# Rotary halves swapped by a TensorE permutation matmul instead of by DMA

## The reference, cut to what matters

```python
def rotary(x):                       # x: (batch, token, head, 64)
    ...
    x1, x2 = xf[..., : d // 2], xf[..., d // 2 :]
    return jnp.concatenate([x1 * cos - x2 * sin, x1 * sin + x2 * cos], axis=-1)

rq = rotary(r_q.reshape(B, S, RET_HEADS, RET_QK_DIM))
rk = rotary(r_k.reshape(B, S, RET_HEADS, RET_QK_DIM))
y_ret = head_groupnorm(retention(rq, rk, ...))
```

## Time and profile before

| | |
|---|---|
| median of three runs | 1784.98 us (1782.87 to 1786.29) |
| the profiled execution's own time | 1786.29 us |
| its span | 1784.6 us |
| PE busy | 1704.8 us, 96% of the span |
| DVE, ACT, POOL busy | 463.6, 387.2, 105.0 us |
| DMA, whole span | 502.70 MB, 282 GB/s |

### The profile page before, as it was taken

One profiled execution on the slowest core, in us unless ns is written; L12 is line 12 of the kernel. 1 busy time (PEld: TensorE's weight loads), 2 busy tenths in 40 slices (PEclk: granted clock), 3 DMA queues, 4 the chain that ended last, 5 costly groups with the idle time before them and its releaser, 6 DMA issues.

```text
span 1784.6 us, 36430 instructions
## 1 busy us (share of the span) xinstructions
PE 1704.8 (96%) x15726; PEld 954.2 (53%) x15726; DVE 463.6 (26%) x868; ACT 387.2 (22%) x604; POOL 105.0 (6%) x191
## 2 busy tenths in 40 slices
PE   7989999999999997999999999999999999999986
PEld 5767887888788766434434343434333343343333
DVE  4354527325544344561000000000000000010015
ACT  5464323333334325001001010100000000000011
POOL 0011000000000011000000000000000000000012
PEclk9999999999999999899999999999999999999998
DMA  7202421233225332999999999999999999999995
GB/s 240 71 24 76 155 98 39 87 102 142 95 94 190 118 95 102 407 396 399 390 410 397 411 398 411 399 409 399 411 410 400 411 409 403 410 408 404 411 417 218
DMA packets 105105, 502.70 MB, mean 282 GB/s; under 512 B 11191, under 2 KB 21575, under 8 KB 55457
## 3 DMA queue, kind: packets, MB, share of 16 engines
q1 hardware_dynamic: 83904, 461.40, 65.5%
q0 software_dynamic: 8192, 26.37, 4.8%
q10 hardware_dynamic: 12864, 12.72, 2.0%
HBM read 486.25 MB, written 14.81 MB: 281 GB/s over the span
## 4 chain that ended last, share of the span: by engine, by line
PE 66%; SPq 18%; DMA 8%; DVE 3%; ACT 2%; issue 2%; POOL 1%; another core or an unknown queue 0%; ACTq 0%; DVEq 0%
PE ps L1982 18%; SPq L504 18%; PE ps L2006 9%; PE ps L1669 9%; PE ps L1671 9%; PE ps L1670 9%; DMA work<-in_w_exp_in 7%; PE ps L1766 1%; PE ps L1813 1%; PE ps L1833 1%; PE ps L486 1%; PE ps L1940 1%; PE ps L1973 1%; PE ps L1950 1%; DMA raw<-in_w_in 1%
## 5 line engine op out<-in xcount | busy, mean ns | idle before, releaser
L1982 PE MATMUL ps<-ring,moe 128*32 128x512 f32 x3808 | 416.2, 594 | 3.2 <-DMA ring<-in_w_exp_in 3.2
L1982 PEld LDWEIGHTS ps<-ring,moe 128*32 128x32 f32 x3808 | 115.6, 110 | 289.7 <-issue 257.2
L1564 DVE TENSOR_SCALAR moe<-ps 128x768 f32<-128x768 f32 (+1 forms) x32 | 28.0, 874 | 847.4 <-PE ps L1982 847.4
L2006 PE MATMUL ps<-ring,moe 128*32 128x256 f32 x3648 | 202.6, 379 | 0.2 <-DMA ring<-in_w_exp_out 0.2
L1095 DVE TENSOR_TENSOR wl<-raw,wh 128x1024 fp32r<-128x1024 f32 x104 | 126.0, 1224 | 250.5 <-ACT wh L746 250.5
L746 ACT ACTIVATE wh<-raw 128x1024 fp32r<-128x1024 f32 x104 | 109.0, 1057 | 244.1 <-PE ps L1671 243.5
L2006 PEld LDWEIGHTS ps<-ring,moe 128*32 128x32 f32 x3648 | 110.8, 110 | 82.5 <-DMA ring<-in_w_exp_out 1.0
L1669 PE MATMUL ps<-oph,wh 128*128 128x512 f32 x384 | 150.9, 393 | 2.4 <-DVE work L1227 1.6
L1670 PE MATMUL ps<-opl,wh 128*128 128x512 f32 x384 | 149.7, 390 | 0.0
L1671 PE MATMUL ps<-oph,wl 128*128 128x512 f32 x384 | 149.6, 390 | 0.0
L988 ACT ACTIVATE moe<-ps 128x768 f32<-128x768 f32 (+1 forms) x32 | 23.8, 744 | 579.2 <-DVE moe L1564 579.2
(11 more groups left out here) (327 smaller groups left out, 1686.2 us busy)
## 6 DMA issues: line engine op xcount, KB each, us to landing
ring<-in_w_exp_in SPq DMA_DIRECT2D x172, 1024.0 KB, 28.0
ring<-in_w_exp_out SPq DMA_DIRECT2D x86, 1024.0 KB, 28.9
moe<-in_w_exp_in SPq DMA_DIRECT2D x43, 1024.0 KB, 28.1
work<-in_w_exp_in SPq DMA_DIRECT2D x41, 1024.0 KB, 28.0
raw<-in_w_in SPq DMA_DIRECT2D x26, 1024.0 KB, 5.4
work<-in_w_exp_out SPq DMA_DIRECT2D x22, 1024.0 KB, 29.8
moe<-in_w_exp_out SPq DMA_DIRECT2D x20, 1024.0 KB, 27.9
raw<-in_w_ckv SPq DMA_DIRECT2D x8, 1024.0 KB, 5.0
```

Source lines behind the costliest of these rows:

```text
L1564: nc.vector.tensor_scalar(act_n[:, 0:g], ps[:, 0:g, 256:512].rearrange("p j (n a) -> p j a n", a=2), 1.0 - LIMIT, 1.0 + LIMIT, ALU.max, AL ...
L1982: ins = nc.tensor.matmul(ps[32 * s:32 * s + 32, j, :], xt[:, k, 32 * j:32 * j + 32], w[:, s, :, :], start=False, stop=(k == KT - 1), tile_ ...
L2006: ins = nc.tensor.matmul(y_bank(s, j), at[:, a, j, q, :], w[:, a, s, :], start=False, stop=(q == W2 - 1 and a == 1), tile_position=(0, 32 ...
```

## The change

POOL's eight swap DMAs, their semaphores and the buffers `q_swap` and `k_swap` are gone. A tenth constant matrix, `rot_swap` (128 x 128, loaded with the two matrices of stick-breaking attention, so that this load is 192 KB and no longer 128 KB), has one entry of 1 or -1 in each column; multiplied with a tile of q or k it gives the swapped halves with their signs, and the sine table loses its signs. PE does this product for the eight tiles, in plain float32, right behind `rk` and ahead of `rv0`, into banks 4 to 7: tiles 0 to 3 are q, tiles 4 to 7 are k, and tile `u` of k waits until DVE has finished the sum of tile `u - 4` in the same bank. All eight stand behind a wait for ACT's last eviction of `rk` and one for the last low part of the stick-breaking output (`o_lo`). DVE takes one tile at a time: the product of the swapped tile, read from PSUM, with the sine into a scratch tile of two (`rot_tmp`), the product with the cosine, a wait for both, and the sum. ACT's wait at the first gate tile is gone. The constants behind the new matrix move up by one place.

```diff
-    sine = np.concatenate([-np.sin(ang), np.sin(ang)])
-    rot = np.stack([np.tile(np.cos(ang), (4, 1)), np.tile(sine, (2, 1))]).astype(np.float32)
+    rot = np.stack([np.tile(np.cos(ang), (4, 1)), np.tile(np.sin(ang), (4, 1))]).astype(np.float32)
...
+    for m in range(P):
+        d = m % 64
+        mats[3, m + 32 if d < 32 else m - 32, m] = -1.0 if d < 32 else 1.0
...
-        q_swap, k_swap = view(8704, 4, T), view(10752, 4, T)
+        rot_tmp = view(1024, 2, T)
...
-            pool.dma_start(w_(14976, 2 * P).rearrange("p (c n) -> p c n", c=2),
-                           c_mats[1:3].rearrange("c p n -> p c n")).then_inc(in_neg, 16)
+            pool.dma_start(w_(14976, 3 * P).rearrange("p (c n) -> p c n", c=3),
+                           c_mats[1:4].rearrange("c p n -> p c n")).then_inc(in_neg, 16)
...
-            for n, (dst, src) in enumerate(((q_swap, q_r), (k_swap, k_r))):
-                pool.wait_ge(tile_out["act"], 16 + 4 * n)
-                for b in range(4):
-                    a = 32 * (b ^ 1)
-                    pool.dma_start(dst[32 * b:32 * b + 32], src[a:a + 32]).then_inc(swapped[n], 16)
...
-                    if n == 0 and t == 0:
-                        act.wait_ge(rot_out, 8)
...
-            for n, (part, other) in enumerate(((q_r, q_swap), (k_r, k_swap))):
-                dve.wait_ge(swapped[n], 64)
-                for u in range(4):
-                    nc.vector.tensor_tensor(other[:, u, :], other[:, u, :], sine, ALU.mult).then_inc(rot_part, 1)
-                    nc.vector.tensor_tensor(part[:, u, :], part[:, u, :], cosine, ALU.mult).then_inc(rot_part, 1)
-                for u in range(4):
-                    dve.wait_ge(rot_part, 8 * n + 2 * u + 2)
-                    nc.vector.tensor_tensor(part[:, u, :], part[:, u, :], other[:, u, :], ALU.add).then_inc(rot_out, 1)
+            for u in range(8):
+                v = (q_r, k_r)[u // 4][:, u % 4, :]
+                dve.wait_ge(rot_done, u + 1)
+                if u >= 2:
+                    dve.wait_ge(rot_out, u - 1)
+                chain(nc.vector.tensor_tensor(rot_tmp[:, u % 2, :], ps[:, 4 + u % 4, :], sine, ALU.mult))
+                chain(nc.vector.tensor_tensor(v, v, cosine, ALU.mult))
+                chain.wait()
+                nc.vector.tensor_tensor(v, v, rot_tmp[:, u % 2, :], ALU.add).then_inc(rot_out, 1)
...
             project("rk", op_h, op_l)
+            pe.wait_ge(tile_out["act"], 20)
+            for u in range(8):
+                if u >= 4:
+                    pe.wait_ge(rot_out, u - 3)
+                elif u == 0:
+                    pe.wait_ge(o_lo, PAIRS)
+                nc.tensor.matmul(ps[:, 4 + u % 4, :], rot_swap, (q_r, k_r)[u // 4][:, u % 4, :], start=True,
+                                 stop=True).then_inc(rot_done, 1)
             for name in ("rv0", "rv1", "rg0"):
                 project(name, op_h, op_l)
...
             pe.wait_ge(rot_out, 8)
-            pe.wait_ge(o_lo, PAIRS)
             retention_scores(0)
```

More of the change, by code:

```diff
@@ L147, in constant_tables @@
     i = np.arange(P)
-    mats = np.zeros((9, P, P), np.float32)
+    mats = np.zeros((10, P, P), np.float32)
     mats[0] = np.eye(P)
@@ L151, in constant_tables @@
     mats[2] = -1.0
[L152 to L155, removed]
+    for m in range(P):
+        d = m % 64
+        mats[3, m + 32 if d < 32 else m - 32, m] = -1.0 if d < 32 else 1.0
+    mats[4] = i[:, None] < i[None, :]
+    mats[5] = 1.0
+    mats[6] = i[None, :]
+    mats[7] = (i[:, None] % NE) == (i[None, :] % NE)
     for g in (2, 3):
@@ L164, in constant_tables @@
                 break
-        mats[10 - g, :, order] = np.arange(32 * g)[:, None]
+        mats[11 - g, :, order] = np.arange(32 * g)[:, None]
     inv = np.float32(10000.0) ** (-np.arange(0, 64, 2, dtype=np.float32) / np.float32(64))
     ang = (np.arange(T, dtype=np.float32)[None, :] * inv[:, None]).astype(np.float32)
-    sine = np.concatenate([-np.sin(ang), np.sin(ang)])
-    rot = np.stack([np.tile(np.cos(ang), (4, 1)), np.tile(sine, (2, 1))]).astype(np.float32)
+    rot = np.stack([np.tile(np.cos(ang), (4, 1)), np.tile(np.sin(ang), (4, 1))]).astype(np.float32)
     u = np.arange(2 * P)[None, :] - i[:, None]
@@ L242, in view @@
             return w_(a, tiles * n).rearrange("p (t n) -> p t n", t=tiles)
-        neg_from, neg_ones = (w_(14976 + P * n, P) for n in range(2))
+        neg_from, neg_ones, rot_swap = (w_(14976 + P * n, P) for n in range(3))
         x_nat = view(0, TT, D)
@@ L390, in layer_kernel @@
         ln_done, neg_ready, soft_hi, soft_lo = (sem(n) for n in ("ln_done", "neg_ready", "soft_hi", "soft_lo"))
-        swapped, rot_part, rot_out = [sem("q_swapped"), sem("k_swapped")], sem("rot_part"), sem("rot_out")
+        rot_done, rot_out = sem("rot_done"), sem("rot_out")
         sc_done, sc_out, ro_done, ro_out = (sem(n) for n in ("sc_done", "sc_out", "ro_done", "ro_out"))
@@ L616, in _ @@
             pool.wait_ge(xo_done, 2 * XH)
-            pool.dma_start(mats2, c_mats[3:7].rearrange("c p n -> p c n")).then_inc(in_moe, 16)
+            pool.dma_start(mats2, c_mats[4:8].rearrange("c p n -> p c n")).then_inc(in_moe, 16)
             pool.dma_start(names["brt"], b_router[0].partition_broadcast(P)).then_inc(in_moe, 16)
@@ L638, in _ @@
             pool.wait_ge(rt_ready, 3)
-            pool.dma_start(mats2[:, 0:2, :], c_mats[7:9].rearrange("c p n -> p c n")).then_inc(in_fill, 16)
+            pool.dma_start(mats2[:, 0:2, :], c_mats[8:10].rearrange("c p n -> p c n")).then_inc(in_fill, 16)
             def gather_rows(g):
```

## The result

The changed kernel takes 1797.47 us (median of 8 runs, 1791.52 to 1800.96) against 1786.12 us for the kernel before (8 runs): a ratio of 1.0054, 95% interval 1.0041 to 1.0067. In two later sets of runs it was 1.0062 (1.0045 to 1.0078) and 1.0058 (1.0039 to 1.0077). The change costs 10 to 12 us. One more execution of the changed kernel, taken with the first measurement, ran for 2953.05 us at a mean granted clock of 0.557; it belongs to a slow state of the chip, and no number here uses it. The profiled execution has a span of 1794.9 us, 10.3 more than before.

A forecast was written before the change was run, and what follows sets the result against it. PE was taken to bound the rotary stretch, with no idle time. Swaps of 6.9 us and waits of 3.9 us made 10.8 us, added to the 1784.98 us median for 1795.8 us; range 1792.5 to 1799.5 us.

The forecast's parts named there:

- The sum: PE from rk to rv0: 6.9 us of swaps plus 3.9 us of waiting, 10.8 us slower.
- Rival B: Swap stretch on PE: the clock falls as well, 1.5 us more, 12.3 us slower; chance 0.42 together with D.
- D: PE's queue at the swaps: each hand-over costs 0.3 us more, 12.3 us slower; chance 0.42 together with Rival B.
- A: The sum as it stands: 10.8 us slower, TensorE's clock unchanged; chance 0.52.
- What bounds: Rotary stretch, 166.8 to 254 us: PE never idle, so its time is paid at once; removing the swap DMAs gives 0.
- Step 1: PE behind rk: waits for ACT's last copy, first swap at 189.62 us; 0.8 us of waiting.
- Step 2: Each swap on PE, a float32 product of 128 x 128 with 512 columns: 0.86 us.
- Steps 3 and 4: DVE's rotation: starts about 1.2 us after the first swap, then takes 1.93 us for each tile.
- Steps 5 and 6: Last swap on PE waits for DVE's fourth sum; rv0 starts at 199.6 us, a loss of 10.8 us.
- What is queued behind: Work after the rotary step: DVE's next splits 2.5 us later, with 20 us of cover; 0 put on each.
- Rival C: Last stage: the DMA-limited stream of expert weights hides PE's 10.8 us, time unchanged at 1785.0; chance 0.05.

The follow-up runs named there:

- e1: The kernel before plus eight float32 matmuls on PE behind rk whose results nobody reads: ratio 1.0023, loss 6.9 us in its trace.
- e2: The changed kernel with q's swaps moved behind rv0 and k's behind rv1, DVE's rotation moved with them: ratio 1.0030, loss 6.9 us.
- e5: The changed kernel with only k's swaps moved behind rv0 and DVE's rotation of k behind rv0's splits: ratio 1.0048, loss 7.9 us.
- e3: The changed kernel without DVE's product with the cosine, so the rotation is incomplete: ratio 1.0036, loss 8.5 us.
- e4: The changed kernel with one-pass swaps from the upper halves of the float32 words, read as bfloat16: ratio 1.0057, loss 10.9 us.
- before_again: The kernel before, unaltered, run again for a trace on the chip of the later experiments: ratio 1.0017 to itself, loss 0.0 us.
- after_look: The changed kernel, unaltered, for one more trace on the chip of the later experiments: ratio 1.0058, loss 10.9 us.
- after_again: The changed kernel, unaltered, run again beside the first experiments: ratio 1.0062 to the kernel before, loss 10.9 us.

## Why the prediction was right

The sum was 10.8 us, 1795.8 us in all; 10.9 us were lost at the scores, and the median moved by 11.4 in the first measurement, 12.1 and 11.1 in the others. The measured 1797.47 us is 1.7 more than 1795.8; 1.1 of this is that the kernel before came out at 1786.12 over eight runs and not at 1784.98. As a number it lies nearer to the 1797.3 of rivals B and D than to A's; it is the traces that decide for A.

- What bounds: PE had no idle time there, so matmul time is paid at once. e1 shows it: 6.9 us for eight matmuls that nobody waits for. Of the removed swap DMAs and DVE's wait of 3.44 us for them nothing came back, as said (e1 and e2 lose the same).
- Step 1, the wait for ACT: ACT's copy ran from 189.32 here, and the first swap started at 189.98, 1.08 us behind the last matmul of `rk`. Predicted 1.07 (189.62 - 188.55). Its price by itself is 1.0 us (e5 less e2), where the prediction had 0.8.
- Step 2, the swap: 6.9 us for eight (e1), so 0.86.
- Steps 3 and 4: DVE started 1.23 us behind the first swap (1.2), and its period is 1.93 us. The product with an operand in PSUM took 0.69 us, that without 0.68, so no run shows an extra cost of a source in PSUM.
- Steps 5 and 6: `rv0`'s second product came 11.35 us behind the last matmul of `rk`, 0.45 before: 10.9 us. e3 shows that DVE's period is in this term with a factor of four.
- What is queued behind: DVE came to its next splits at 206.63, 2.8 us later than 203.81, of which 0.35 is the later end of `rk` in this execution; 2.5 was predicted. PE never waited for a low part in `rv0` to `rg0`.
- What was off: the text had the last four swaps 1.93 us apart and PE idle for about 3 us before them; it was the last three, and 2.3 us, since tile 4 found its bank free. That does not touch the sum, which goes by the last swap alone. The idle time on record (2.3 and 0.7 us for ACT) is less than the 4.0 us that the waits cost, because each record lasts past the point at which a next one could have started: 1.12 us for a swap of 0.86.
- Rival B, the clock: the grant was 1.00 from 193 to 206 us in all three traces of the changed kernel and in e3, and fell to 0.50 in e4. Where it fell it cost 1.0 us in `rv0`, and 1.5 was predicted. The 1.5 to 1.7 us of the prediction are what the grants of 0.56 and 0.51 leave undone in 3.40 us. It put PE at 1.8 of 3.4 us busy, between the 1.61 of 3.40 us that came ahead of the 0.51 and the 2.10 of 3.40 us behind which 1.00 stayed, and so called B nearly even; PE was busy for 2.27 of 3.41 us, more than in the row that held. If the busy share decides, B's chance was put too high, by a busy time that was put too low; that it decides was an estimate from those rows. The changed kernel and e4 agree with it, and do not prove it: with PE busy for 2.27 of 3.41 us the granted clock was 1.00, and in e4, with 1.00 and then 1.90 of 4.00 us, it was 0.86 and then 0.50, but the type of the operands differs too.
- Rival C, the last stage hides it: no. The last load was issued 10.8 us later and the span grew by 10.3. Up to the router nothing is given back (429.0 us from the scores, before and after). Whether one to three microseconds of a loss are given back behind it stays open; the totals of e1 to e3 (1.1 to 2.4 us less than their losses) and the traces of before_again and after_look point that way, those of e5 and of the changed kernel do not, and an unaltered kernel was off by 4.5 us in the median.
- D, slower hand-overs: no; each is within 0.1 us of its row.

No version here beats the kernel before: the eight float32 swaps without any wait (e2) cost 6.9 us, and the DMAs that they replace cost PE nothing. One-pass swaps in e2's place were not run; eight at the 0.23 us by which projection matmuls follow one another would be an estimate of 1.8 us, at a loss of precision.

## What to carry to other kernels

Here PE had no idle time, so data moved with a matmul cost the matmul's full time (6.9 us for eight, e1), while the DMAs, whose result PE wanted 50 us later, cost it nothing: look for cover before you replace a transfer. When a short exchange between two engines is put into a busy queue, work out the period of the slower partner and how many of its turns stand ahead of the queue's next own work: here four turns of 1.93 us, and taking away PE's share of it (e4) gained 1.1 us of the exchange and lost 1.0 of it again behind a granted clock of 0.50. And if the exchange must be there, put it where the other engine's result is already old (e2): that alone gave back 4.0 us.

## What the runs showed of the hardware that was not expected

At one place the granted clock fell in some executions of a kernel and not in others. Between the scores and the router it fell to 0.50 at 490 us for 3.4 us in the first trace of the changed kernel, and was 1.00 in after_again and after_look, which are the same kernel; in before_again it was 0.50 for 6.8 us from 476 us, and in the first trace of the kernel before 1.00 throughout. In e1 to e5 it fell to 0.50 too, from a point between 485 and 489 us, for 3.4 us (e5: 6.8). The stretch from the scores to the router took 429.0 to 429.1 us without such a fall and 1.5 to 2.9 us more in every trace that has one. The time of a run went with its mean granted clock, at about 1.5 us for each 0.001, and this is a good part of the 5 to 15 us over which the runs of one kernel spread on one chip.

The last stage may also differ from chip to chip. From the first matmul of the router to the end it took 1090.8 to 1091.4 us in the four traces of one chip (after_again, e1, e2, e3) and 1095.5 to 1099.0 us in the four of the other; the same kernel took 1091.4 us in after_again and 1095.5 in after_look. These are single traces, but the difference is as large as some of the losses here, so a loss is only to be read against the kernel before on the same chip.

Shorter work of PE between waits came with a price in the one kernel that has it: in e4, where PE was busy for 1.00 and then 1.90 of 4.00 us and in the changed kernel for 2.27 of 3.41, the granted clock fell to 0.50 in the exchange, and the matmuls behind it ran at that clock until 201.7 us. Its operands are bfloat16 and those of the changed kernel float32, so these runs don't show which of the two brought the fall.
